# Value products alternating between the two heads of a pair, and one weight chunk loaded ahead of a store's wait and split by ScalarE and VectorE

## The reference, cut to what matters

```
x = layer_norm(x, ln_in_g, ln_in_b)
h = einsum('bsd,de->bse', x, w_in)           # 2816 columns, split into ten parts
ya = mixer_spatial_gating(...)               # gMLP
yb = mixer_conformer_conv(...)               # starts with  y = a * sigmoid(b)
yc = mixer_window_attention(q, k, v, ...)    # 8 query heads of 64, 2 key heads, blocks of 128
y = einsum('bse,ed->bsd', concatenate([ya, yb, yc], -1), w_out)
x = layer_norm(DEEPNORM_ALPHA * x + y, post_ln_g, post_ln_b)
```

## Time and profile before

| what | us |
|---|---|
| median of 3 runs | 1254.55 (1253.87 to 1254.64) |
| the profiled execution | 1250.48 |
| its span | 1248.6 |
| TensorE busy | 1208.9 |
| VectorE busy | 660.4 |
| GpSimd busy | 469.4 |
| ScalarE busy | 349.6 |

### The profile page before, as it was taken

One profiled execution on the slowest core, in us unless ns is written; L12 is line 12 of the kernel. 1 busy time (PEld: TensorE's weight loads), 2 busy tenths in 40 slices (PEclk: granted clock), 3 DMA queues, 4 the chain that ended last, 5 costly groups with the idle time before them and its releaser, 6 DMA issues.

```text
span 1248.6 us, 15984 instructions
## 1 busy us (share of the span) xinstructions
PE 1208.9 (97%) x5977; PEld 966.7 (77%) x5977; DVE 660.4 (53%) x1220; ACT 349.6 (28%) x710; POOL 469.4 (38%) x449
## 2 busy tenths in 40 slices
PE   6999999999999999999998999889999999999995
PEld 5777878788888878787786788779888886667784
DVE  4325355422465203167767946856694525445468
ACT  6211110100022112446565421321111144433211
POOL 3224222232545223444665654314322324443343
PEclk9999999999999999999999999989999999999998
DMA  6131121243311223100114412222121110051112
GB/s 216 56 131 43 36 75 34 101 169 101 75 49 53 68 68 106 60 26 24 54 39 144 166 46 70 83 97 69 51 68 35 59 35 35 5 190 34 37 50 118
DMA packets 72702, 92.84 MB, mean 74 GB/s; under 512 B 12721, under 2 KB 51849, under 8 KB 72114
## 3 DMA queue, kind: packets, MB, share of 16 engines
q1 hardware_dynamic: 63906, 87.62, 21.0%
q10 hardware_dynamic: 8720, 4.20, 1.2%
HBM read 74.45 MB, written 18.92 MB: 75 GB/s over the span
## 4 chain that ended last, share of the span: by engine, by line
PE 88%; DVE 6%; POOL 2%; DMA 1%; issue 1%; ACT 1%; SPq 0%; ACTq 0%; POOLq 0%; DVEq 0%
PE bank L829 22%; PE bank L831 21%; PE bank L830 21%; PE bank L1078 3%; PE bank L1095 3%; PE wide L1251 2%; PE wide L930 2%; PE bank L1232 2%; PE wide L1241 2%; PE wide L1088 2%; DVE res L1908 1%; DMA wraw<-in_w_in 1%; PE bank L1038 1%; PE bank L1049 1%; PE bank L1026 1%
## 5 line engine op out<-in xcount | busy, mean ns | idle before, releaser
L610 POOL CAST whi<-wraw 128x2048 fp32r<-128x2048 f32 x32 | 60.6, 1894 | 448.9 <-PE bank L831 361.1
L829 PE MATMUL bank<-u_hi,wlo 128*128 128x512 f32 x512 | 202.7, 396 | 2.9 <-DVE u_lo L1349 2.9
L831 PE MATMUL bank<-u_hi,whi 128*128 128x512 f32 x512 | 200.1, 391 | 0.0
L830 PE MATMUL bank<-u_lo,whi 128*128 128x512 f32 x512 | 199.9, 390 | 0.0
L612 POOL TENSOR_TENSOR wlo<-wraw,whi 128x2048 fp32r<-128x2048 f32 x33 | 155.9, 4725 | 3.1 <-ACT whi L2230 0.5
L829 PE MATMUL bank<-x_hi,wlo 128*128 128x512 f32 x320 | 129.2, 404 | 7.2 <-POOL wlo L612 6.4
L830 PE MATMUL bank<-x_lo,whi 128*128 128x512 f32 x320 | 125.5, 392 | 0.0
L831 PE MATMUL bank<-x_hi,whi 128*128 128x512 f32 x320 | 125.5, 392 | 0.0
L829 PEld LDWEIGHTS bank<-u_hi,wlo 128*128 128x128 f32 x512 | 96.6, 189 | 25.9 <-DVE u_lo L1349 4.0
L831 PEld LDWEIGHTS bank<-u_hi,whi 128*128 128x128 f32 x512 | 96.5, 188 | 20.4
L830 PEld LDWEIGHTS bank<-u_lo,whi 128*128 128x128 f32 x512 | 96.5, 188 | 20.2 <-issue 0.7
(11 more groups left out here) (330 smaller groups left out, 2430.7 us busy)
## 6 DMA issues: line engine op xcount, KB each, us to landing
wraw<-in_w_in SPq DMA_DIRECT2D x27, 1024.0 KB, 5.4
wraw<-in_w_out SPq DMA_DIRECT2D x12, 1024.0 KB, 5.1
xr<-in_x SPq DMA_DIRECT2D x8, 512.0 KB, 8.7
hst<-in_x SPq DMA_DIRECT2D x4, 1024.0 KB, 6.0
hpool<-hst SPq DMA_DIRECT2D x4, 1024.0 KB, 4.1
smz<-mzs SPq DMA_DIRECT2D x16, 256.0 KB, 2.1
wraw<-nmax ACTq DMA_DIRECT2D x32, 128.0 KB, 3.0
h<-hpool SPq DMA_DIRECT2D x4, 1024.0 KB, 6.8
```

The lines of the kernel that those rows point to most:

```text
L610: g_.tensor_copy(whi[w % 2][:, :, :], wraw[:, :, :]).then_inc(s["w_hi"], 1)
L829: pe.matmul(ps, al, bh, start=(k == 0), stop=False)
L830: pe.matmul(ps, ah, bl, start=False, stop=False)
L831: return pe.matmul(ps, ah, bh, start=False, stop=(k == nk - 1))
```

## The change

Three edits. In `weigh` both waits now stand ahead, and the loop over key blocks is outside the loop over heads. SyncE issues the load of `W_BB` before the store of tile 4 instead of after it. The split of `W_BB` leaves GpSimd: ScalarE makes its high part between `square_h(5)` and `root_h(5)`, and VectorE its low part between `sum_h` of tile 7 and the statistics of tile 5. GpSimd waits for the first eight transposes ahead of its memsets.

```diff
@@ block.sync
             for t in range(NT):
-                if t == 5:
-                    wt(W_2 + 1)
+                if t == 4:
+                    wt(W_BB)
                 sp_.wait_ge(s["v_xh"], t + 1)
                 sp_.dma_start(res_d[:, t, :], h2[:, t, :])...
@@ block.gpsimd
             split(W_2)
-            split(W_BB)
             g_.wait_ge(s["o_sp0"], 48)
+            g_.wait_ge(s["t_x2"], 8)
             g_.memset(glu[:, :, 0:PAD2], 0.0).then_inc(s["g_init"], 1)
@@ block.tensor, weigh(x)
-                for i in range(2):
-                    pe.wait_ge(s[("a_pT", "v_pT")[i]], x + 1)
-                    for b in range(nb):
+                pe.wait_ge(s["a_pT"], x + 1)
+                pe.wait_ge(s["v_pT"], x + 1)
+                for b in range(nb):
+                    for i in range(2):
                         mm = pe.matmul(ps[64 * i:64 * i + 64, 0:P], vt[...], pT[:, i, ...],
                                        start=(b == 0), stop=(b == nb - 1))
@@ block.vector
             sum_h(3, 7)
+            ve.wait_ge(s["w_hi"], W_BB + 1)
+            ve.tensor_tensor(wlo[W_BB % 2][:, :, :], wraw[:, :, :], whi[W_BB % 2][:, :, :].bitcast(F32), ALU.subtract
+                             ).then_inc(s["w_lo"], 1)
             for t in range(5, NT):
@@ block.scalar
+            def high_w(w):
+                ac.wait_ge(s["l_wraw"], 16 * (w + 1))
+                ac.wait_ge(s["t_gemm"], done(w - 2))
+                ac.activation(whi[w % 2][:, :, :], wraw[:, :, :], ACT.Copy).then_inc(s["w_hi"], 1)
...
             square_h(4)
-            (the same three lines, written out for W_2)
+            high_w(W_BA)
             high_x2(*range(8))
             root_h(4)
             for t in range(5, NT):
                 square_h(t)
+                if t == 5:
+                    high_w(W_BB)
                 root_h(t)
```

More of the change, by code:

```diff
@@ L2227, in _ @@
             square_h(4)
-            ac.wait_ge(s["l_wraw"], 16 * (W_2 + 1))
-            ac.wait_ge(s["t_gemm"], done(W_2 - 2))
-            ac.activation(whi[W_2 % 2][:, :, :], wraw[:, :, :], ACT.Copy).then_inc(s["w_hi"], 1)
+            high_w(W_BA)
             high_x2(*range(8))
```

## The result

| | before | after |
|---|---|---|
| median of 4 runs | 1254.21 (1252.36 to 1254.64) | 1237.73 (1235.63 to 1240.95) |
| the profiled execution | 1250.48 | 1235.63 |
| its span | 1248.6 | 1233.7 |

The ratio is 0.9874, interval 0.9848 to 0.9899, so the change takes off 12.7 to 19.1 us. The forecast was 14.5 us and 1240.0 (1236.5 to 1245.5). The two profiled executions differ by 14.9 us, and the whole of it lies where it was expected. The first transpose of `h2` tiles starts at 784.73 before and at 784.76 after; up to there the two kernels do the same.

The account below looks back on a forecast made before the run. TensorE, busy for 97% of the span, was taken to bound the kernel. Alternation 6.3 us plus chunk 8.2 us gave 14.5 us, from median 1254.55 to 1240.0; own range 1238 to 1242, with rivals and a larger gain 1236.5 to 1245.5.

Parts of the forecast that it names:

- Part A: Attention's value products: alternating two heads' records takes 24 long steps from 1.07 to 0.81 us, saving 6.3 us.
- the forecast rate of 0.0545: Value products: each alternating record beyond eight costs 0.0545 us, taken from lines 1192 and 1206.
- Rival 3: Value products: changing column half between neighbours drains the array, making it slower, 1272 us with p = 0.1; 2%.
- The wait moved ahead: Value products: waiting for `v_pT` before head 0's first product costs 0, since VectorE's copy ends 3 us earlier.
- Part B: Join of the blocks: early load and moved split of `W_BB` start the transposes at 819.0 instead of 827.2, saving 8.2 us.
- the subtraction: Join: VectorE's low part of `W_BB`, 128x2048, costs 2.4 us, bounds 2.1 and 4.63.
- What would be late next: Join: TensorE then waits for tile 7, normed on VectorE, from 818.3 to 819.0, 0.6 us.
- the 4.9 us: Join: with GpSimd silent, VectorE's centring of tile 6 and scaling of tile 5 get 0.98 + 3.91 us shorter.
- (1) no pairing: Value products: the alternation gives nothing, only 8.2 us come, time 1246.3; 6%.
- (2) VectorE late: Join: VectorE late with tile 7 through a 4.63 us subtraction or GpSimd collisions, losing 2.2 to 4.9 us; 10%.
- (4) the load: Join: load of `W_BB` goes out early but lands after 801 behind other transfers; 2 us give 1242; 3%.

Follow-up runs that it names:

- e1: Kernel before with only the new alternating order of the value products in `weigh`; median 1244.73 us, ratio 0.9943.
- e5: Kernel before with only both waits of the value products set ahead, order of the products unchanged; 1251.47 us in one run.
- e8: Changed kernel with VectorE's subtraction for the low part of `W_BB` made twice; 1238.01 us in one run.
- e7: Changed kernel with the gain multiply of tile 5 (second half) moved from VectorE to GpSimd; median 1234.97 us, ratio 0.9877.
- e3: Changed kernel with the low part of `W_BB` given back to GpSimd, load still early; 1238.47 us in one run.
- e4: Changed kernel with both parts of `W_BB` given back to GpSimd, load still early; 1235.48 us in one run.
- e10: The changed kernel run again, unaltered; median 1236.34 us, ratio 0.988.
- e9: Changed kernel with the load of `W_BB` back behind the store of tile 4; 1246.72 us in one run.

## Why the prediction was right

**Part A, 6.3 us for 6.45.** The price of 12 alternating records, 0.81 us, came from two other lines and was exact. The records of a long step span 0.603 us, about what six records of one half do (0.597); the forecast rate of 0.0545 is half the 0.109 between records of one half. One reading was wrong, and the sum did not use it: the prediction took the 0.48 us between a long and a short step for four records of a lone head at 0.12 each. By the starts, 0.262 us of it is the later entry of head 1 (0.275 instead of 0.013), and 0.218 is two more of its records at 0.109. Rival 3 was priced with these 0.12.

The prediction read the Trainium skill's page "TensorE: Matmul & The Clock Gate", section "Part 3: Packing small matmuls — row/col tiling", as saying that two heads can't run beside each other, which would have given 0; the trace of before spoke against it and e1 decided. That reading was narrower than the section, whose table also has three matmuls packed by columns at 2.38 times the speed. Its sentence that matmuls start strictly in program order doesn't fit this trace, if the starts above are read rightly. The wait moved ahead cost 0, as e5 shows alone.

**Part B, 8.2 us for 8.38.** The load landed in time, ScalarE's cast started at 799.56 (799.6 forecast), `w_lo` was there at 803.8 (804.0). The one term that was off is the subtraction: 2.2 us to the next instruction instead of 2.4, within its bounds, and the hole was 0.49 for 0.6. Its price of 2.4 was extrapolated from two sizes with 0.60 per 512 elements, but the two rows are two different operations: 0.69 is a TENSOR_TENSOR, 1.29 a SCALAR_TENSOR_TENSOR. Within TENSOR_TENSOR it is 2.29 - 0.69 = 1.60 for 1536 elements, 0.53 per 512.

**What would be late next** was named rightly: VectorE with tile 7. e8 and e7 show it from both sides. That rests on the 4.9 us that VectorE got back from GpSimd's silence; without them the hole would have been over 5 us, by an estimate from 4.9 and 0.49. The Trainium skill's rule on the ports ("SBUF — State Buffer", "Who interferes with whom") was right to 0.2 us in four new places: the 4.98 us in e3 and the 2.07, 3.36 and 5.46 us in e4.

**The rivals.** (1) no pairing: excluded by e1. (2) VectorE late: no, but e3 and e4 show that it would have been real with the split left where it was, 1.7 to 3.0 us (of the 3.0, 1.1 is clock). (3) drains: excluded, with a change of half at every second record the starts lie 0.0548 us apart (0.603 over 11 distances), as at line 1206 (0.0546). (4) the load: it landed ahead of 799.56.

**The time.** The median came 2.3 us below the forecast. From the traces the gain is 14.9, not 16.5; e10, beside its own runs of before, has 14.6 by the medians. The profiled execution took 1235.6 for the 1236.0 forecast. The rest is that the prediction put the median 4.1 us above it, as in its three runs of before, and it came out at 2.1. That is the scatter of both kernels, and not a part of the change.

## What to carry to other kernels

Where outputs use half of the array's columns, put records of the two halves close together; six records of one half ahead of the other cost a quarter of the time here, four cost nothing, and two waits set ahead of both cost nothing if the data are ready. When TensorE waits for a chunk, look first for the wait in the load's own queue that has nothing to do with it: moving the load over one store gave 6.7 of 8.4 us. Before giving work to GpSimd because it is idle, look at what VectorE reads at that time; the extra VectorE work was cheaper than GpSimd's free help.

## What the runs showed that I had not expected

**A hole doesn't always cost the clock, and not by its length alone.** TensorE in the same stretch behind its hole, columns as in the earlier trace rows, first e3 (hole 2.69 us), then e8 (3.03):

```profile
822.00:830.00 8.00, 7.79 (x41) 0.82 0.74 216
```

```profile
822.00:830.00 8.00, 7.34 (x46) 1.00 0.82 248
```

The longer hole kept 1.00 and the shorter one did not; e3 lost 1.1 us by it (206.3 us from the transposes to the first value product in e8 and the others without a slow clock behind the transposes, 207.4 in e3). In e9 the first hole, 3.5 us between starts, was followed by 1.00 and the second, 4.15, by 0.75 (from 827 to 832). Behind the hole of 6.8 us between starts the clock fell in all three kernels that have it, and not for equally long: 9 distances of 0.427 us between starts in before, 11 in e1, 12 in e5, each 0.2 us dearer than at 1.00. I had counted the price as fixed. Where between 2.4 and 6.8 us the clock is safe can't be said from these runs.

**Most of the scatter between executions is ahead of the join, in work that is the same in all kernels.** The mark lies between 782.96 (e4) and 788.18 us (e9). Most of it is the clock again. One place is a stretch where TensorE runs without a hole: before, and after.

```profile
410.00:425.00 15.00, 15.00 (x93) 0.89 0.32 105
```

```profile
410.00:425.00 15.00, 15.00 (x86) 0.77 0.24 80
```

The other executions have 0.66 to 0.89 in this stretch. Added up over all that lies ahead of the mark, the clock is at 0.50 for 3.4 us in e4, whose mark is the earliest, for 6.8 us in the seven executions with marks from 783.91 to 785.26, for 10.2 in the four from 785.96 to 787.82, and for 13.7 in e9, the latest. At 0.427 us a matmul instead of 0.227 the 10.2 us more of e9 against e4 cost about 4.8 of the 5.2 us between their marks; within a group up to 1.9 us stay without a cause. The kernel before and e5 repeat to 0.6 us from the mark to the end, the changed kernel and e10 to 0.02. So a trace compared from a mark tells half a microsecond, where the median of four runs leaves 2 to 3.
